# A hybrid attention layer on Trainium2: the gate row summed earlier, the last output block in halves, and loops over pairs of heads written out

## The chip, the cores and the metric

The kernel runs on one core of a Trainium2 chip. The metric is the device time of one execution in microseconds, as a median over runs. Five engines work side by side, each on its own list of instructions, and meet only at semaphores: TensorE (PE, with its weight loads shown as PEld), VectorE (DVE), ScalarE (ACT), GpSimd (POOL) and SyncE (SP), whose queue issues nearly all DMA transfers.

## The reference: what is computed

One decoder layer on x of shape (1, 2048, 1024), all in float32:

```
ada = silu(c) @ w_ada + b_ada;  shift, scale, gate = split(ada, 3)
h = rms_norm(x, norm_w) * (1 + scale) + shift
q_sb, k_sb, v_sb, g_sb, c_q, c_kv, k_rope, g_mla = split(h @ w_in)
A: stick-breaking attention, 8 heads of 64:
   w[t,s] = beta[t,s] * prod over s<j<t of (1 - beta[t,j]), s < t;  beta = sigmoid(q k / 8)
   o_sb = (w @ v) * silu(g_sb)
B: causal softmax attention, 8 heads, q and k of 96 (64 + 32 rotary), v of 64,
   q and kv lifted from latents of 384 and 256, per-head RMS norms of q and k
   o_mla = (softmax(q k / sqrt(96)) @ v) * silu(g_mla)
out = x + gate * (concat(o_sb, o_mla) @ w_out)
```

`gate` is one row of 1024 numbers: silu(c) times the last third of `w_ada`, plus the last third of `b_ada`.

## The kernel before

Four stages follow each other, the first two closed by a barrier of all engines. To keep float32 accuracy at the speed of the rounded type, most operands are split into a high part (a rounded copy, by ScalarE or GpSimd) and a low part (the operand less its high part, by VectorE or GpSimd), and a product is made as three matmuls: high by high, low by high, high by low.

**Features** (`features`, to 416.2 us). The normalised input is turned, split and multiplied with the columns of q, k and both gates. Beside it VectorE forms the products of the gate row (`gate_row`, lines 549 to 560): partition p of the tile `keep` (128 x 1024) holds the sum over k of silu(c)[k*128+p] times row k*128+p of `w_ada`. The sum over the 128 partitions and the bias are still missing.

**Tokens** (`tokens`, lines 723 to 1366, 416.2 to 797.8 us). For each of 16 blocks of 128 tokens: values, latents, lifted q and k, norms, rotary turn, and their transposes. It opens with the weights: SyncE issues the loads (lines 891 to 912), ScalarE casts eight blocks of `w_tok` (line 1003) and then five blocks of the lifting weights (line 1007), VectorE makes the low parts (lines 1108, 1115), and TensorE's first product (`project_v`, line 1278) takes the eight blocks one by one as their low parts come (`s_wl`). The PSUM tile `pq` is first written by the transposes of `latents` for block 0.

**Attention** (`attend`, from 797.8 us). Heads are taken in four pairs, the variable `it`. In both parts a Python planner (`Plan`, `Turns`) lays down the order in which every engine goes through the pair: *units* or *pieces* of 128 x 512 scores, and *turns*, one block of 128 keys for 512 queries. A turn passes from engine to engine through rings of four or eight tiles.

The stick-breaking part (`attend_sb`): TensorE makes scores (line 1799), ScalarE takes a sigmoid (line 1635), VectorE a running product (line 1713); then TensorE transposes (line 1828), ScalarE copies out of PSUM (line 1646), GpSimd makes the high part and the low part for three turns of four (lines 1607 and 1609) and TensorE multiplies with the values (lines 1843, 1844). A pair has 80 units and 80 turns. The helper `pairs` (line 1496) runs pair 0 as written-out code and pairs 1 to 3 as passes of one counted loop, in which each engine jumps back on its own:

```python
def pairs(eng, body):
    body(0, True)
    with eng.Fori(1, PAIRS) as it:
        body(it, False)
```

Waits inside the loop compare a semaphore with a value computed in a register from `it`.

The softmax part (`attend_mla`): TensorE makes scores twice, once to find row maxima (line 2250, `piece`; VectorE reduces them, line 2162) and once transposed (line 2287); ScalarE exponentiates twice (lines 2109, 2110), GpSimd makes the low part (line 2083), VectorE adds up (line 2201), TensorE multiplies with the values (lines 2303, 2304). At the end of a group of 512 queries, ScalarE copies the scale (line 2132), GpSimd multiplies with the SiLU gate (line 2094), VectorE with the scale (line 2224), and high and low parts are stored (line 2033). Its `run` writes out pairs 0 and 3 and loops over pairs 1 and 2, so each engine jumps back once. The code runs straight on from the stick-breaking part, and the first pieces are mixed into its last turns.

**Output** (`output`). Sixteen blocks of 128 rows, last rows first. For each, 48 matmuls into one of two pairs of PSUM banks (line 2453), VectorE multiplies with `keep` (line 2432), GpSimd adds x (line 2422), SyncE stores. SyncE issues the loads of block n+2 (four for the mixed heads, one for x) after the store of block n. Before the first multiply the gate row is finished here: after the last weights of the softmax, TensorE multiplies `keep` with a matrix of ones into the banks of block 1 (line 2438), which sums over partitions and spreads the sum at once; `sync` loads the bias (line 2402) after the last product with the values, behind the loads of x for block 0 and of both inputs of block 1; VectorE adds the two into `keep` (line 2427). TensorE's block 1 waits for that, since its banks hold the sum.

## Time and profile before

| | us |
|---|---|
| median of 3 runs (lowest, highest) | 2006.79 (1998.55, 2008.7) |
| the profiled execution | 2009.26 |
| its span in the trace | 2007.5 |
| PE busy | 1862.4 (93%) |
| DVE busy | 1251.5 (62%) |
| POOL busy | 1029.5 (51%) |
| ACT busy | 950.9 (47%) |
| output stage, from about 1803 us | 204.5 |

Busy shares over the whole span hide that the stages differ; the rows further down give them by stage. In a timeline row the bracket gives the idle time of that engine before the operation and what the profile takes to have ended it. Branches and register instructions are not counted as busy.

### The profile page before, as it was taken

The page shows a single profiled execution, that of the slowest core. Times are in us where ns is not written, and L with a number is a line of the kernel's source. Part 1 is how long each engine was busy: PE and PEld are TensorE (multiplying, and loading weights), DVE is VectorE, ACT ScalarE, POOL GpSimd, SP SyncE. Part 2 cuts the span into 40 slices and gives each one's busy share as a digit, 9 for nine tenths or more (in the row PEclk, how much of TensorE's full clock was granted, in tenths as well). Part 3 has the DMA queues.
Part 4 walks back from the last instruction along what each step waited for, and adds up shares of the span by engine and source line. Part 5 has one row for each costly group of instructions (what it writes and reads, how often), then busy time and mean ns, then how long its engine had stood idle before and what let it go on. Part 6 is the DMA issues. An engine that isn't in the chain of part 4 may idle for free.

```text
span 2007.5 us, 31970 instructions
## 1 busy us (share of the span) xinstructions
PE 1862.4 (93%) x9757; PEld 1545.8 (77%) x9757; DVE 1251.5 (62%) x1875; ACT 950.9 (47%) x1892; POOL 1029.5 (51%) x1038
## 2 busy tenths in 40 slices
PE   7999999979999994799998989799999999987998
PEld 4888888859999993587777767588887887876786
DVE  4742222135555554799989899788988889872010
ACT  2521111133333332477776767577777777770000
POOL 3410000003333433299998989777877878771122
PEclk9999999989999996799999999899999999988999
DMA  7696522344555544631618053514550545315654
GB/s 274 225 315 201 170 89 89 116 179 158 182 180 191 185 160 138 159 85 50 161 38 194 22 148 68 128 46 86 108 123 23 126 94 103 118 43 163 188 183 147
DMA packets 224836, 273.83 MB, mean 136 GB/s; under 512 B 14000, under 2 KB 161744, under 8 KB 219328
## 3 DMA queue, kind: packets, MB, share of 16 engines
q1 hardware_dynamic: 221088, 266.58, 46.8%
q10 hardware_dynamic: 3616, 5.77, 1.0%
q8 instruction: 49, 0.80, 0.2%
q14 instruction: 83, 0.68, 0.1%
HBM read 159.06 MB, written 109.05 MB: 134 GB/s over the span
## 4 chain that ended last, share of the span: by engine, by line
PE 26%; issue 13%; POOL 9%; DVE 5%; DMA 3%; ACT 2%; SPq 1%; POOLq 0%; ACTq 0%; DVEq 0%
PE at_high L2287 8%; POOL sb_wh L1607 3%; PE at_low L2250 3%; DVE sb_w L1713 3%; PE at_b L2303 3%; PE at_low L1799 3%; POOL sb_wl L1609 2%; PE at_b L2304 2%; DMA out_x<-in_x 2%; POOL out_o L2422 2%; PE at_b L1828 2%; POOL wl L2083 1%; PE at_b L2315 1%; PE at_b L1843 1%; PE at_b L1844 1%
## 5 line engine op out<-in xcount | busy, mean ns | idle before, releaser
L2083 POOL TENSOR_TENSOR wl<-w,wh 128x512 fp32r<-128x512 f32 (+1 forms) x320 | 377.6, 1195 | 101.5 <-ACT wh L2110 95.6
L1609 POOL TENSOR_TENSOR sb_wl<-sb_wf,sb_wh 128x512 fp32r<-128x512 f32 (+2 forms) x240 | 286.4, 1193 | 19.2
L1713 DVE TENSOR_TENSOR_SCAN sb_w<-kp,sb_w,at_high 128x512 f32<-128x512 f32 x192 | 245.4, 1278 | 28.1 <-ACT kp L1635 12.6
L2109 ACT ACTIVATE w<-at_high 128x512 f32<-128x512 f32 (+1 forms) x320 | 170.8, 534 | 117.0 <-PE at_high L2287 58.5
L2162 DVE TENSOR_REDUCE nmx<-at_low 128x1 f32<-128x512 f32 (+2 forms) x320 | 191.6, 600 | 7.2 <-PE at_low L2250 4.3
L1635 ACT ACTIVATE kp<-at_low 128x512 f32<-128x512 f32 (+3 forms) x320 | 169.0, 531 | 32.7 <-PE at_low L1802 12.3
L1607 POOL CAST sb_wh<-sb_wf 128x512 fp32r<-128x512 f32 (+2 forms) x240 | 145.7, 607 | 57.3 <-ACT sb_wf L1646 56.8
L663 PE MATMUL pt_po<-h_hi,pt_wl 128*128 128x512 f32 x432 | 170.3, 394 | 0.0
L662 PE MATMUL pt_po<-h_lo,pt_wh 128*128 128x512 f32 x432 | 169.3, 392 | 0.0
L2110 ACT ACTIVATE wh<-at_high 128x512 fp32r<-128x512 f32 (+1 forms) x320 | 169.1, 529 | 0.0
L661 PE MATMUL pt_po<-h_hi,pt_wh 128*128 128x512 f32 x432 | 168.1, 389 | 0.0
L1843 PE MATMUL at_b<-sb_wh,values 128*128 128x512 f32 (+1 forms) x320 | 145.1, 454 | 19.8 <-POOL sb_wl L1609 19.4
L1799 PE MATMUL at_low<-keys,q_hi 128*128 128x512 f32 (+3 forms) x320 | 131.2, 410 | 32.4 <-DMA q_lo<-qk_sb 20.1
L85 POOL MEMSET tk_ident<- 128x128 f32 x1 | 0.2, 204 | 298.0 <-POOLq L64 298.0
L2201 DVE TENSOR_TENSOR at_b<-at_b,w 128x512 f32<-128x512 f32 x168 | 116.8, 695 | 29.6 <-ACT w L2109 26.1
L2250 PE MATMUL at_low<-keys,q_hi 96*128 96x512 f32 (+2 forms) x320 | 124.5, 389 | 10.6 <-DVE nmx L2162 10.5
L2287 PE MATMUL at_high<-q_hi,keys 97*128 97x512 f32 (+1 forms) x320 | 126.0, 394 | 2.5 <-ACT wh L2110 1.9
L1646 ACT ACTIVATE sb_wf<-at_b 128x512 f32<-128x512 f32 (+2 forms) x160 | 88.4, 553 | 77.4 <-PE at_b L1828 75.9
L2303 PE MATMUL at_b<-wh,values 128*128 128x512 f32 (+1 forms) x320 | 124.0, 387 | 0.7 <-POOL wl L2083 0.6
L1828 PE MATMUL at_b<-ident,sb_w 128*128 128x128 f32 x732 | 117.6, 277 | 3.9 <-DVE sb_wl L1722 3.5
L1799 PE MATMUL at_low<-keys,q_lo 128*128 128x512 f32 (+3 forms) x320 | 121.0, 378 | 0.0
L2422 POOL TENSOR_TENSOR out_o<-out_y,out_x 128x1024 f32<-128x1024 f32 x16 | 38.2, 2387 | 159.9 <-DVE out_y L2432 151.4
(266 smaller groups left out, 4658.1 us busy)
## 6 DMA issues: line engine op xcount, KB each, us to landing
qk_mla<-tk_th SPq DMA_DIRECT2D x64, 192.0 KB, 2.1
qk_mla<-tk_tl SPq DMA_DIRECT2D x64, 192.0 KB, 2.4
whole<-in_w_ada SPq DMA_DIRECT2D x8, 1024.0 KB, 14.2
pt_w<-in_w_feat SPq DMA_DIRECT2D x16, 512.0 KB, 6.0
qk_sb<-pt_oh SPq DMA_DIRECT2D x32, 256.0 KB, 3.1
qk_sb<-pt_ol SPq DMA_DIRECT2D x32, 256.0 KB, 4.0
hT<-h_hi SPq DMA_DIRECT2D x16, 512.0 KB, 4.7
hT<-h_lo SPq DMA_DIRECT2D x16, 512.0 KB, 6.2
```

The lines of the kernel that those rows point to most:

```text
L662: nc.tensor.matmul(bank[:], wh[s][:, k, :], hl[:, k, cols_q], start=False, stop=False)
L663: mm = nc.tensor.matmul(bank[:], wl[s][:, k, :], hh[:, k, cols_q], start=False, stop=(k == KD - 1))
L1607: nc.gpsimd.tensor_copy(wh[i][:, lo:GW], wf[i][:, lo:GW]).then_inc(s_phi, 1)
L1609: nc.gpsimd.tensor_tensor(wl[i][:, lo:GW], wf[i][:, lo:GW], wh[i][:, lo:GW].bitcast(F32), ALU.subtract).then_inc(s_plo, 1)
L1713: nc.vector.tensor_tensor_scan(kept, keeps, beside[:, 0:b - a], 1.0 if u["n"] == 0 else w[u["g"]][:, u["r"], b:b + 1], ALU.mult, ALU.bypas ...
L1799: mm = nc.tensor.matmul(out, buf[x][hp][:, q], buf["kk"][hp][:, u["a"]:u["z"]], start=(k == 0), stop=(not masked and k == 1))
L2083: nc.gpsimd.tensor_tensor(wl[i][:, cols], w[i][:, cols], wh[i][:, cols].bitcast(F32), ALU.subtract).then_inc(s_lo, 1)
L2109: nc.scalar.activation(w[i][:, cols], zt[x % 2][:, cols], ACT.Exp).then_inc(s_w, 1)
L2162: nc.vector.tensor_reduce(nmx[pc["n"] % 2][:, pc["r"], pc["c"]:pc["c"] + 1], zn[p % 2][:, 0:pc["width"]], AX.X, ALU.max, negate=True).then ...
L2250: mm = nc.tensor.matmul(zn[p % 2][:, 0:width], qh[hp][0:QK, i * P:(i + 1) * P], kh[hp][0:QK, pc["c"] * GW:pc["c"] * GW + width], start=Tru ...
L2287: mm = nc.tensor.matmul(zt[x % 2][:, lo:GW], a[hp][0:KP, keys], b[hp][0:KP, g * GW + lo:(g + 1) * GW], start=(k == 0), stop=(k == 2 and no ...
L2303: nc.tensor.matmul(out, vj, wh[x % RING][:, lo:GW], start=tn["first"], stop=False)
```

## The change

1. *Gate row.* The sum over partitions moves to the start of the token stage. SyncE loads the last third of `b_ada` as two rows of 512 on one partition, into tiles not yet used, right behind the two head norms and ahead of the weight loads. TensorE, before its first product, adds for each half of the row `ones(128x128) x keep` and `ones(1x128) x bias` in PSUM (`pq`), and ScalarE, between its two groups of weight casts, copies the finished row back into `keep`. The transposes of block 0 wait for that copy. In the output stage the two matmuls, the bias load and the addition go; block 1 waits for the last softmax weights instead.
2. *Loads.* A new `load_second` issues the loads of x for blocks 0 and 1 and of the mixed heads for block 1 as soon as the last scores are made, after the second group's store of the last pair, no longer behind all stores.
3. *Last block.* Block 15 is multiplied in two halves of 512 columns, each through all of k. VectorE multiplies each half with the gate row; GpSimd adds x to the first, VectorE itself to the second; each half is stored by itself.
4. *Pairs.* `pairs`, `run` and both `sync` bodies are Python loops over the four pairs: every pair is written out on every engine, and waits compare with constants. The order of operations within and between pairs is as before.

```diff
--- before.py
+++ after.py
@@ -741,6 +741,7 @@
         dv = m.sb("dv", [P, H * HD])
+        ones = m.sb("ones", [P, P])
         vt = m.sb("vt", [P, H, 2, HD], F32R)
@@ -800,7 +801,13 @@
+        bias = [dv[0:1, :], ln[0:1, 0:512]]
+
         s_ident = m.sem("ident")
+        s_ones = m.sem("ones")
+        s_bias = m.sem("bias")
+        s_gsum = m.sem("gate_sum")
+        s_gate = m.sem("gate")
         s_const = m.sem("const")
@@ -890,6 +897,8 @@
             sp.dma_start(gk[:], t["k_head_norm"].partition_broadcast(P)).then_inc(s_head, 16)
+            for j in range(2):
+                sp.dma_start(bias[j], t["b_ada"][2 * D + j * 512:2 * D + (j + 1) * 512].unsqueeze(0)).then_inc(s_bias, 16)
             for k in range(SLOTS, NS):
@@ -946,6 +955,7 @@
         def _(pool):
+            nc.gpsimd.memset(ones[:], 1.0).then_inc(s_ones, 1)
             make_identity(nc, pool, ident, s_ident)
@@ -1001,6 +1011,8 @@
                 nc.scalar.activation(wh[:, k, :], raw(k % NS), ACT.Copy).then_inc(s_wh, 1)
+            act.wait_ge(s_gsum, 1)
+            nc.scalar.activation(keep[:].rearrange("p (j n) -> p j n", j=2), pq[:], ACT.Copy).then_inc(s_gate, 1)
             for j in range(NW):
@@ -1296,6 +1308,8 @@
                 pe.wait_ge(s_ln, 2 * m_ + 2)
+                if isinstance(m_, int) and m_ == 0:
+                    pe.wait_ge(s_gate, 1)
@@ -1362,6 +1376,14 @@
+            pe.wait_ge(s_ones, 1)
+            for j in range(2):
+                if j == 0:
+                    pe.wait_ge(s_bias, 32)
+                cols = slice(j * 512, (j + 1) * 512)
+                nc.tensor.matmul(pq[:, j, :], ones[:], keep[:, cols], start=True, stop=False)
+                mm = nc.tensor.matmul(pq[:, j, :], ones[0:1, :], bias[j], start=False, stop=True)
+            mm.then_inc(s_gsum, 1)
             pe.wait_ge(s_ident, 2)
@@ -1493,11 +1515,10 @@
-    def pairs(eng, body):
-
-        body(0, True)
-        with eng.Fori(1, PAIRS) as it:
-            body(it, False)
+    def pairs(body):
+
+        for it in range(PAIRS):
+            body(it, it == 0)
@@ -1577,10 +1598,8 @@
-        body(0, True, False)
-        with sp.Fori(1, PAIRS - 1) as it:
-            body(it, False, False)
-        body(PAIRS - 1, False, True)
+        for it in range(PAIRS):
+            body(it, it == 0, it == PAIRS - 1)
         store(PAIRS - 1, 0)
...
@@ -1673,7 +1692,7 @@
                 for n, wraps in plan.due(x, after):
-                    if not (isinstance(it, int) and not 0 <= it - wraps < PAIRS):
+                    if 0 <= it - wraps < PAIRS:
                         body(it - wraps, n)
...
@@ -1993,21 +2012,19 @@
             at_it, at_hp = it + h // 2, h % 2
-            if isinstance(at_it, int) and not 0 <= at_it < PAIRS:
+            if not 0 <= at_it < PAIRS:
                 continue
-    def run(eng, steps, tail):
+    def run(steps, tail):
-        body(0)
-        with eng.Fori(1, PAIRS - 1) as it:
+        for it in range(PAIRS):
             body(it)
-        body(PAIRS - 1)
         for x in range(TAIL + 1):
@@ -2065,11 +2082,11 @@
                     output.load_first(sp)
-
-        body(0, True, False)
-        with sp.Fori(1, PAIRS - 1) as it:
-            body(it, False, False)
-        body(PAIRS - 1, False, True)
+                if last and n == 1:
+                    output.load_second(sp)
+
+        for it in range(PAIRS):
+            body(it, it == 0, it == PAIRS - 1)
         store(PAIRS - 1, G - 1)
...
@@ -2382,6 +2397,12 @@
+    def load_second(sp):
+        sp.wait_ge(*softmax.scored)
+        load_x(sp, 0)
+        load_mix(sp, 1)
+        load_x(sp, 1)
+
     def split_high(act, k):
@@ -2394,23 +2415,22 @@
     def sync(sp):
-        sp.wait_ge(*softmax.scored)
-        load_x(sp, 0)
-        load_mix(sp, 1)
-        load_x(sp, 1)
-        sp.wait_ge(*softmax.pv)
-        sp.dma_start(bgate[:], t["b_ada"][2 * D:3 * D].partition_broadcast(P)).then_inc(s_bgate, 16)
         for stored in softmax.stored:
             sp.wait_ge(s_o, n + 1)
+            if n == NB - 1:
+                sp.dma_start(out[0, rows(n), halves[0]], o[n % 2][:, halves[0]]).then_inc(s_st[n % 2], 16)
+                sp.wait_ge(s_end, 1)
+                sp.dma_start(out[0, rows(n), halves[1]], o[n % 2][:, halves[1]]).then_inc(s_st[n % 2], 16)
+                break
             sp.dma_start(out[0, rows(n), :], o[n % 2][:]).then_inc(s_st[n % 2], 16)
-            sp.wait_ge(s_st[b], 16 * NB // 2)
+            sp.wait_ge(s_st[b], 16 * (NB // 2) + 16 * b)
@@ -2419,44 +2439,54 @@
             reached(pool, s_st[b], 16 * (n // 2))
-            nc.gpsimd.tensor_tensor(o[b][:], y[b][:], x[b][:], ALU.add).then_inc(s_o, 1)
+            cols = halves[0] if n == NB - 1 else slice(0, D)
+            nc.gpsimd.tensor_tensor(o[b][:, cols], y[b][:, cols], x[b][:, cols], ALU.add).then_inc(s_o, 1)
     def vector(dve):
-        dve.wait_ge(s_gate, 1)
-        dve.wait_ge(s_bgate, 16)
-        nc.vector.tensor_tensor(keep[:], po[1][:], bgate[:], ALU.add).then_inc(s_keep, 1)
-        dve.wait_ge(s_keep, 1)
         for n in range(NB):
             reached(dve, s_o, n - 1)
+            if n == NB - 1:
+                for j, cols in enumerate(halves):
+                    dve.wait_ge(s_mm, n + 1 + j)
+                    nc.vector.tensor_tensor(y[n % 2][:, cols], po[n % 2][:, cols], keep[:, cols], ALU.mult).then_inc(s_y, 1)
+                dve.wait_ge(s_y, NB + 1)
+                dve.wait_ge(s_x[n % 2], 16 * (n // 2) + 16)
+                reached(dve, s_st[n % 2], 16 * (n // 2))
+                nc.vector.tensor_tensor(o[n % 2][:, cols], y[n % 2][:, cols], x[n % 2][:, cols], ALU.add).then_inc(s_end, 1)
+                break
             nc.vector.tensor_tensor(y[n % 2][:], po[n % 2][:], keep[:], ALU.mult).then_inc(s_y, 1)
     def tensor(pe):
-        pe.wait_ge(*softmax.weighed)
-        for j in range(2):
-
-            mm = nc.tensor.matmul(po[1][:, j * 512:(j + 1) * 512], ones[:], keep[:, j * 512:(j + 1) * 512],
-                                  start=True, stop=True)
-        mm.then_inc(s_gate, 1)
         pe.wait_ge(*softmax.max)
             if n == 1:
-                pe.wait_ge(s_keep, 1)
+                pe.wait_ge(*softmax.weighed)
             reached(pe, s_y, n - 1)
+
+            def products(k, js):
+                for l, wx in ((0, wh), (1, wh), (0, wl)):
+                    for j in js:
+                        mm = nc.tensor.matmul(po[b][:, halves[j]], ms[b][l][:, k, :], wx[k][:, halves[j]],
+                                              start=(k == 0 and l == 0 and wx is wh),
+                                              stop=(k == KD - 1 and wx is wl))
+                return mm
+
+            if n == NB - 1:
+                for j in range(2):
+                    for k in range(KD):
+                        mm = products(k, (j,))
+                    mm.then_inc(s_mm, 1)
+                break
             for k in range(KD):
                     pe.wait_ge(s_wl, k + 1)
-                for l, wx in ((0, wh), (1, wh), (0, wl)):
-                    for j in range(2):
-                        mm = nc.tensor.matmul(po[b][:, j * 512:(j + 1) * 512], ms[b][l][:, k, :],
-                                              wx[k][:, j * 512:(j + 1) * 512],
-                                              start=(k == 0 and l == 0 and wx is wh),
-                                              stop=(k == KD - 1 and wx is wl))
+                mm = products(k, (0, 1))
             mm.then_inc(s_mm, 1)
-    return Output(sync, gpsimd, vector, tensor, load_first, split_high, split_low)
+    return Output(sync, gpsimd, vector, tensor, load_first, load_second, split_high, split_low)
...
```

## Rows read from the trace of the kernel before

**Rows 1.** Windows by stage: length; busy PE, PEld, DVE, ACT, POOL; PEclk, DMA, GB/s

```profile
797.80:1300.00 502.20, 447.43 (x2521) 351.06 (x2521) 437.39 (x488) 342.17 (x693) 422.77 (x490) 0.95 0.45 105
1300.00:1803.00 503.00, 485.91 (x2664) 412.33 (x2665) 436.42 (x750) 373.14 (x754) 396.38 (x336) 0.98 0.38 89
```

**Rows 2.** Timeline, GpSimd, pair starts: start, length, operation [idle before <-releaser]

```profile
947.26 0.61 POOL L1607 CAST sb_wh<-sb_wf 128x512 fp32r<-128x512 f32 x1
...
1061.07 0.74 POOL L1609 TENSOR_TENSOR sb_wl<-sb_wf,sb_wh 128x256 fp32r<-128x256 f32 x1
1065.83 0.61 POOL L1607 CAST sb_wh<-sb_wf 128x512 fp32r<-128x512 f32 x1 [4.02 <-ACT sb_wf L1646]
...
1182.22 0.61 POOL L1607 CAST sb_wh<-sb_wf 128x512 fp32r<-128x512 f32 x1 [3.99 <-ACT sb_wf L1646]
```

**Rows 3.** Timeline of ScalarE after its jump back

```profile
1028.88 0.28 ACT L1635 ACTIVATE kp<-at_low 128x128 f32<-128x128 f32 x1 [2.13 <-issue]
```

**Rows 4.** Timeline of GpSimd behind ScalarE's jump back

```profile
1029.90 0.61 POOL L1607 CAST sb_wh<-sb_wf 128x512 fp32r<-128x512 f32 x1 [0.87 <-ACT sb_wf L1646]
...
1034.18 0.61 POOL L1607 CAST sb_wh<-sb_wf 128x512 fp32r<-128x512 f32 x1 [0.38 <-ACT sb_wf L1646]
...
1040.69 0.61 POOL L1607 CAST sb_wh<-sb_wf 128x512 fp32r<-128x512 f32 x1 [0.36 <-ACT sb_wf L1646]
```

**Rows 5.** Timeline of ScalarE in the softmax stage: pair ends and eleventh turns

```profile
1425.31 0.59 ACT L2132 ACTIVATE scale<-at_b 64x512 f32<-64x512 f32 x1 [0.50 <-PE at_b L2323]
...
1443.63 0.59 ACT L2110 ACTIVATE wh<-at_high 128x512 fp32r<-128x512 f32 x1
...
1548.62 0.59 ACT L2132 ACTIVATE scale<-at_b 64x512 f32<-64x512 f32 x1 [0.50 <-PE at_b L2323]
...
1568.63 0.59 ACT L2110 ACTIVATE wh<-at_high 128x512 fp32r<-128x512 f32 x1
...
1693.68 0.59 ACT L2110 ACTIVATE wh<-at_high 128x512 fp32r<-128x512 f32 x1
```

**Rows 6.** Timeline of VectorE, the same operation in two pairs

```profile
1428.88 0.68 DVE L2224 TENSOR_TENSOR om<-om,scale 128x512 f32<-128x512 f32 x1
...
1677.04 1.74 DVE L2224 TENSOR_TENSOR om<-om,scale 128x512 f32<-128x512 f32 x1
```

**Rows 7.** Timeline of TensorE, start of the output stage

```profile
1802.87 3.10 PE L2438 MATMUL at_high<-gate_row,ones 128*128 128x512 f32 x4
...
1816.27 0.61 PE L2453 MATMUL at_low<-out_wl,out_ms 128*128 128x512 f32 x2
1826.75 2.05 PE L2453 MATMUL at_high<-out_wh,out_ms 128*128 128x512 f32 x4 [9.87 <-DVE gate_row L2427]
```

**Rows 8.** Timeline of VectorE in the output stage

```profile
1825.38 1.22 DVE L2427 TENSOR_TENSOR gate_row<-at_high,out_bgate 128x1024 f32<-128x1024 f32 x1 [12.47 <-DMA out_bgate<-in_b_ada]
...
1840.69 1.22 DVE L2432 TENSOR_TENSOR out_y<-at_high,gate_row 128x1024 f32<-128x1024 f32 x1 [12.83 <-PE at_high L2453]
1851.57 1.23 DVE L2432 TENSOR_TENSOR out_y<-at_low,gate_row 128x1024 f32<-128x1024 f32 x1 [9.65 <-PE at_low L2453]
...
1999.45 1.23 DVE L2432 TENSOR_TENSOR out_y<-at_high,gate_row 128x1024 f32<-128x1024 f32 x1 [9.65 <-PE at_high L2453]
```

**Rows 9.** Windows, the stretch at the lower clock in the output stage

```profile
1819.00:1832.60 13.60, 5.85 (x14) 4.68 (x15) 2.45 (x2) 0.00 (x0) 2.36 (x1) 0.50 0.56 176
```

**Rows 10.** Timeline of SyncE's queue in the output stage

```profile
1819.21 0.43 SPq L2402 DMA_DIRECT2D out_bgate<-in_b_ada  x1
```

**Rows 11.** Waits of TensorE from 1840 us on: us, times, longest us

```profile
PE at_high L2453 <- DMA out_ms<-mix_mla: 3.9, 4, 1.8
```

**Rows 12.** Timeline of GpSimd, its last add

```profile
2000.76 2.34 POOL L2422 TENSOR_TENSOR out_o<-out_y,out_x 128x1024 f32<-128x1024 f32 x1 [8.49 <-DVE out_y L2432]
```

**Rows 13.** Timeline of SyncE's queue, start of the token stage

```profile
419.90 1.42 SPq L900 DMA_DIRECT2D region<-in_w_tok  x2
```

**Rows 14.** Timeline of TensorE, start of the token stage

```profile
432.40 1.22 PE L1278 MATMUL tk_pv<-tk_wh,hs 128*128 128x512 f32 x2 [3.75 <-DVE tk_wl L1108]
```

More of the change, by code:

```diff
@@ L2146, in scalar @@
         row(0, 0, 0)
-        run(act, dict(row=row, turn=weights, half=v_low, sums=totals, mh=high), lambda x: output.split_high(act, x))
+        run(dict(row=row, turn=weights, half=v_low, sums=totals, mh=high), lambda x: output.split_high(act, x))
     def rows_ahead(act, i):
@@ L2331, in tensor @@
         to_row(0, 0, 0)
[L2332 removed]
+        run(dict(**pieces(pe), pm=to_row, turn=scores, product=product, spread=spread, sum=over_keys), lambda x: None)
     class done:
```

42 lines of the change are left out of this document (19 added, 23 removed).

## Prediction

> **What bounds the kernel now.** I read first the busy time of each engine in the stretches of the stages, where the reader is to see that the two attention stages are not bound alike. In the stick-breaking stage (797.8 to 1300 us) TensorE, VectorE and GpSimd are all busy 84 to 89% of 502 us; in the softmax stage TensorE leads with 486 of 503 us [rows 1]. An idle microsecond of any engine that the others soon wait for is therefore nearly a microsecond of the kernel there. Then I read the timeline around the places where the counted loops start over. GpSimd's cast for a new pair of heads comes at 947.26, 1065.83 and 1182.22; the last two stand behind 4.02 and 3.99 us of idle time, while the passage from pair 0 (already written out) into the loop, at 947.26, shows none [rows 2]. The rows name ScalarE as releaser, but the gap stands only where GpSimd's loop starts over, and as long both times: I read it as GpSimd's own jump back. ScalarE has such a gap too, 2.13 us with the releaser "issue" [rows 3], and GpSimd then waits for it three times, 0.87+0.38+0.36 us [rows 4]. Third, the output stage: TensorE ends block 0 at 1816.27+0.61 and stands idle 9.87 us for the gate row [rows 7], which VectorE could form only at 1825.38, after 12.47 us for the bias, whose load was issued at 1819.21 [rows 8, 10]. Last, the end: multiply (1.23 us), then GpSimd's add (2.34 us), then the store [rows 8, 12].
>
> **Gate row, removed from the output stage.** Three things go. The wait: 9.87 us. The clock: from 1819.0 to 1832.6 the granted clock was 0.50, the 1.2 GHz level, after TensorE had fallen idle [rows 9], so block 1 took from 1826.75 to the multiply at 1840.69, 13.94 us, where block 2 took 1851.57-1840.69 = 10.88 us [rows 7, 8]; 3.06 us come back if block 1 follows block 0 without a pause. The two matmuls with the ones: 3.10 us ahead of block 0 [rows 7]. Block 0 can move up by that at most, and by less where VectorE's weight splits or a lower clock hold it: 0 to 3.1 us, taken 1.4. Together 9.87+3.06+1.4 = 14.3 us at the end of block 1, which then ends near 1826.4. That needs block 1's own loads early: `load_second` issues them when the last scores are made (about 1795), ahead of the third group's store, which is due only at 1807; they are there long before 1815.5. What is late next: the loads for block n+2 follow the sum of block n. Block 2 had them free while TensorE stood idle; now its loads start near 1819.5 and block 1 ends near 1826.4. The same distance cost block 3 1.8 us, the longest of the four waits of that kind, 3.9 us in all [rows 11]. I give back 1.0 us (0 to 3). Net: -13.3 us.
>
> **Gate row, added to the token stage.** SyncE issues two more loads ahead of the weights. One such issue costs 0.43 us [rows 10], so everything behind them on that queue goes out about 0.8 us later, and with it the weight blocks issued at 419.90 [rows 13], for whose low part TensorE waits 3.75 us at 432.40 [rows 14]. That wait is on the path: +0.8 us. The matmuls: two of the same shape took 3.10 us at the lower level [rows 7]; four take up to 6.2 us there and half of that at the upper. They start when the bias is in, near 419.5, while TensorE otherwise has only as much to do as VectorE's weight splits come in; it catches up in the 3.75 us of idle time before 432.40. So their price is nothing; without that cover it would be 3 us. ScalarE copies the row, 128x1024, about 1 us between two groups of weight casts; queued behind it are those casts and the first copy of values, and TensorE needs neither before its next token block. GpSimd's extra memset (0.2 us for a like one on the page) is done before the bias is in. Bounds 0 to +3, taken +0.8 us.
>
> **Pairs of heads written out, stick-breaking.** Two jumps back go on each engine. GpSimd's: 4.02+3.99 us gross [rows 2]. But the trace shows that part of it is given back: the pair that begins after a stall lasts 1182.22-1065.83 = 116.39 us, the one that begins without lasts 118.57 us [rows 2], both with one stall inside; behind the stall the ring is full and GpSimd runs without waiting. So a stall is worth 4.0-2.2 = 1.8 us net, two 3.6 us. ScalarE's: the three waits that it hands to GpSimd are 1.6 us [rows 4], twice 3.2 us. Sum -6.8 us. Bounds: 3 us (if the waits of rows 4 are mostly the ordinary ones) and 2x4.0+2x2.13 = 12.3 us (nothing given back). Register arithmetic that goes with the loop variable I count at nothing: in the softmax stage a looped pair and a written-out one take 125.00 and 125.05 us [rows 5]. The Trainium skill ("Runtime: NRT & Kernel Launch", Instruction fetch mechanics) says that a jump taken to a target outside the two blocks at hand forces a fetch before work goes on, and that straight code is prefetched mostly hidden. By that rule, the trace agrees with 4.0 and 2.1 us at the jumps and none at 947.26; the sum would be the same.
>
> **The same, softmax stage.** One jump back goes, at 1548.7. A pair without one lasts 1548.62-1425.31 = 123.31 us. From the eleventh turn of one pair to that of the next it is 1568.63-1443.63 = 125.00 us with the jump and 1693.68-1568.63 = 125.05 us without it [rows 5]. So the jump costs 1.7 us, but the following pair lost as much without one: there VectorE's multiply of two SBUF operands took 1.74 us in place of 0.68 [rows 6]. Whether the freed pair runs like the first or like the last I can't tell: -1.7 to 0, and to the loss side +1.7 if another pair falls into that pattern. Taken -0.8 us. The Trainium skill ("SBUF — State Buffer", SBUF: two separate sides) has a rule that speaks against a clean gain here: VectorE with two SBUF inputs and GpSimd hold one port pair exclusively, and the later one waits for the whole instruction. By that rule, the trace agrees with 1.74 against 0.68 us; timing alone decides which pair pays.
>
> **Last block in halves.** From the last matmul to the store: now 1.23 us, then GpSimd's add to 2003.10, 3.65 us after 1999.45 [rows 8, 12]. After: VectorE multiplies half a row (0.7 us) and adds the half itself (two SBUF operands of 128x512, 0.68 us without a neighbour [rows 6]; GpSimd's half is done 5 us earlier), with hand-over 1.5 us: -2.2 us. The last transfer is half as large: 0 to 1 us, no row shows this size, taken 0.4. TensorE's count of matmuls and weight loads is the same in either order. Sum -2.6 us.
>
> **Sum.** -13.3+0.8-6.8-0.8-2.6 = -22.7 us. The profiled execution took 2009.26 us (span 2007.5): 1986.6. From the median of the runs, 2006.79, it is 1984.1. I say 1985.
>
> **Rivals.** (a) The jumps are absorbed or return as other stalls in straight code, and only the output stage gains: 2006.79-15.1 = 1991.7 us. For it: all three engines are near 88%, so the next limit is near. Against: pair 0 of either stage. (b) Nothing is given back in the stick-breaking stage and the softmax pair is freed: 12.3+1.7 for 7.6 us, 1977.7 us. Against: 118.57 and 116.39. (c) The change doesn't do what it says in the output stage: block 1's loads come as late as now (about 1822), TensorE pauses 6.5 us, and the lower clock level stays, 3 us: 1993.6 us. Against: SyncE has nothing else to wait for at 1795. (d) Slower: the code itself becomes the bound. Five pairs that were loop passes are now new code on every engine; if GpSimd stalled in straight code as it does at a jump, 4.0 us, twice in each, that is 40 us against 15.1, 2032 us. It decides from the eighth stall on (25 us above the output's gain). Against: pair 0 of the stick-breaking stage and the last softmax pair run straight without a gap of that kind.
>
> **How the numbers follow.** Forecast 0.60 (its own range 1980 to 1990), (a) 0.17, (b) 0.12, (c) 0.05, (d) 0.03, and 0.03 for mixtures near no change. A measurement here can tell about 0.5%, 10 us, from no change; the runs shown spread from 1998.55 to 2008.7. Faster: all but (d) and the mixtures, and a little of (c): 0.93; same 0.04; slower 0.03. The range takes in (a), (b) and the bounds of the token stage: 1973 to 1996.
>
> **What would show it.** Right: in the changed profile GpSimd's gaps of 4.0 us near 1061 and 1178 are gone, the pairs of the stick-breaking stage are 113 to 114 us apart, block 1 of the output starts within 0.5 us of block 0's end at clock 1.0, and the last store follows TensorE by about 2.2 us. Wrong: gaps of 2 to 4 us on GpSimd or ScalarE inside straight pairs (d), pairs still 116 us or more apart (a), a DMA wait before block 1 (c), or the token stage longer by over 3 us.

## The result, and the profile after

The changed kernel takes 1976.79 us (median of 4 runs, 1971.02 to 1983.54) where the kernel before, on the same chip, takes 2007.74 us (4 runs, 1998.55 to 2008.7). The ratio is 0.9859, with a 95% interval of 0.9832 to 0.9885: 23 to 34 us less. The profiled execution took 1976.82 us with a span of 1975.1, which is 32.4 us less than the span before. The forecast was 22.7 us less, given as 1985 us.

By stage, the windows of after that answer to [rows 1] (length, then busy time of PE, PEld, DVE, ACT and POOL, then granted clock, DMA share, GB/s; moved so that they begin with the same work):

```profile
790.00:1285.00 495.00, 443.51 (x2517) 348.05 (x2517) 436.89 (x487) 342.10 (x691) 423.47 (x489) 0.95 0.46 108
1285.00:1782.00 497.00, 481.73 (x2653) 408.31 (x2653) 433.45 (x745) 371.27 (x752) 397.17 (x336) 0.99 0.39 90
1800.00:1811.00 11.00, 11.00 (x50) 8.90 (x48) 1.22 (x1) 0.00 (x0) 2.39 (x1) 1.00 0.57 173
```

The engines do the same work in the stick-breaking stage (443.5 against 447.4 us of TensorE, 436.9 against 437.4 of VectorE) in less time. What went is idle time. The third line is block 1 of the output: TensorE is busy without a pause and at the upper clock level, where [rows 9] showed 0.50.

GpSimd at the starts of the four pairs, which answers to [rows 2] (start, length, operation, idle time before it and its releaser):

```profile
835.26 0.61 POOL L1626 CAST sb_wh<-sb_wf 128x512 fp32r<-128x512 f32 x1 [38.35 <-ACT sb_wf L1665]
...
944.30 0.61 POOL L1626 CAST sb_wh<-sb_wf 128x512 fp32r<-128x512 f32 x1
...
1056.72 0.61 POOL L1626 CAST sb_wh<-sb_wf 128x512 fp32r<-128x512 f32 x1
...
1169.20 0.61 POOL L1626 CAST sb_wh<-sb_wf 128x512 fp32r<-128x512 f32 x1
```

The casts at 1056.72 and 1169.20 have no bracket: the gaps of 4.02 and 3.99 us are gone. The pairs are 112.42 and 112.48 us apart, where it was 118.57 and 116.39.

VectorE in the output stage, which answers to [rows 8]:

```profile
1800.31 1.22 DVE L2458 TENSOR_TENSOR out_y<-at_low,gate_row 128x1024 f32<-128x1024 f32 x1 [3.03 <-PE at_low L2472]
1811.19 1.22 DVE L2458 TENSOR_TENSOR out_y<-at_high,gate_row 128x1024 f32<-128x1024 f32 x1 [9.65 <-PE at_high L2472]
...
1969.87 0.69 DVE L2452 TENSOR_TENSOR out_y<-at_high,gate_row 128x512 f32<-128x512 f32 x1 [4.65 <-PE at_high L2472]
1970.59 0.69 DVE L2456 TENSOR_TENSOR out_o<-out_y,out_x 128x512 f32<-128x512 f32 x1
```

Blocks 0 and 1 are multiplied 10.88 us apart, the distance of two undisturbed blocks. The last multiply starts at 1969.87. SyncE issues the last store 1.44 us after it, where the last add of before ended 3.65 us after its multiply [rows 8, 12]:

```profile
1966.62 0.34 SPq L2423 DMA_DIRECT2D out<-out_o  x1
1971.31 0.33 SPq L2425 DMA_DIRECT2D out<-out_o  x1
```

**One pair of profiles is not enough.** Cut at the same instructions, the profile after is 1.66 us ahead at the first weight remainder of the token stage already, 415.79 against 417.45 us. The diff changes nothing before that point. Over all fourteen profiles of this study that moment lies between 415.66 and 418.76 us, in kernels whose code is the same up to there (one, e11, has its loops there written out: 417.82). So the terms below are taken as means over profiles that have, or lack, the piece in question.

### The profile page after: what moved, and what is told of

The parts are those of the page before. It is cut to its first block, busy times and chain, and to the rows that moved or that the text cites. A ratio compares the mean times of both kernels' runs of the same rounds, so it can differ in the third digit from the quotient of the medians.

```text
span 1975.1 us, 29422 instructions
## 1 busy us (share of the span) xinstructions
PE 1856.5 (94%) x9761; PEld 1538.4 (78%) x9761; DVE 1251.6 (63%) x1876; ACT 953.3 (48%) x1893; POOL 1031.9 (52%) x1039
## 4 chain that ended last, share of the span: by engine, by line
PE 25%; issue 11%; POOL 10%; DVE 10%; DMA 2%; ACT 1%; SPq 1%; POOLq 0%; ACTq 0%; DVEq 0%
PE at_high L2304 8%; DVE sb_w L1732 6%; POOL sb_wl L1628 4%; PE at_low L2267 3%; POOL sb_wh L1626 3%; PE at_b L2320 3%; PE at_b L2321 2%; POOL wl L2100 2%; PE at_low L1818 2%; DMA out_x<-in_x 2%; POOL out_o L2443 2%; PE at_b L2332 1%; PE at_b L1847 1%; PE at_b L1862 1%; SPq L2386 1%
## 5 line engine op out<-in xcount | busy, mean ns | idle before, releaser
L1863 PE MATMUL at_b<-sb_wl,values 128*128 128x512 f32 (+1 forms) x320 | 117.9, 369 | 0.0
```

## Experiments

Each kernel gets a median and a ratio to the kernel before, timed on the same chip. The medians of before were 2005.63 (e1 to e4), 2004.72 (e5 to e8) and 2006.38 us (e9 to e12). From each profile I also take the same seven distances, starts of instructions read off the timelines:

- **token**: VectorE's first `tk_wl` to TensorE's last high-part matmul (`tk_wh`) into `tk_pv`
- **stick**: ScalarE's first `kp` to GpSimd's last cast `sb_wh`
- **softmax**: GpSimd's first to its last `wl`
- **block 1**: that last `wl` to the multiply of the output's second block
- **blocks**: from there to the multiply of the 15th block
- **tail**: from there to the start of the last instruction on record
- the first moment (**start**), 415.66 to 418.76 us throughout

```
kernel              token   stick  softmax  block 1  blocks   tail    span
before             326.47  482.82   491.92    43.98  147.88  18.90  2007.5
e1_loops_both      326.74  473.64   489.09    42.36  146.88  19.28  1995.2
e2_loops_stick     326.71  473.40   489.78    42.30  146.19  18.99  1993.1
e3_loops_softmax   326.71  480.52   488.36    42.76  146.93  18.90  2000.8
e4_output_part     326.19  480.48   492.44    27.98  145.23  16.22  1983.2
e5_stick_pool      327.12  478.58   493.94    42.26  146.04  18.92  2001.8
e6_stick_scalar    327.06  479.08   487.50    41.43  146.28  19.20  1993.3
e7_gate_old_loads  325.14  484.90   489.47    37.81  147.16  16.18  1997.0
e8_halves_alone    326.97  483.52   488.92    41.44  147.65  16.91  2001.1
e9_warm_only       325.60  481.00   490.12    42.32  146.15  18.99  1999.1
e10_token_small    326.94  473.17   490.12    28.99  146.29  16.25  1974.3
e11_all_loops_out  325.00  474.37   489.06    29.21  146.07  16.48  1975.8
e12_after_again    325.37  473.70   489.63    29.17  146.88  16.08  1974.3
after              325.37  473.93   489.36    28.39  147.32  16.54  1975.1
```

### The loops alone: e1, e2, e3

```
-        body(0, True)
-        with eng.Fori(1, PAIRS) as it:
-            body(it, False)
+        for it in range(PAIRS):
+            body(it, it == 0)
```

This is done on all five engines (SyncE's loop has its last pass apart) in both stages (e1), in the stick-breaking stage (e2) or in the softmax stage (e3).

> The kernel before, with the loops over the pairs written out on all five engines in both attention stages and nothing else changed. By the theory as predicted (each jump gives back about half of its stall, the softmax stage almost nothing): -7.6 us, about 2000.1. By the rival read from the two traces (8.5 us in the stick-breaking stage, 4.3 in the softmax stage): -12.8 us, about 1995. If the loops' part of the difference were a chance of the profiled runs, under 5 us.

> The kernel before, with the pairs written out in the stick-breaking stage alone. As predicted: -6.8 us, about 2000.9; distances of the first casts of pairs on GpSimd 113 to 114 us throughout. By the traces: -8.5 us, about 1999.2, with distances 109, 112.4, 112.5, 115.2.

> The kernel before, with the pairs written out in the softmax stage alone. As predicted: -0.8 us, about 2006.9. By the traces: -4.3 us, about 2003.4. If the 4.3 us of the softmax stage came instead from when that stage starts (the clock in its first turns), the change is the 1.1 to 2.3 us of the jump behind pair 1 alone.

Measured: e1 1995.67 us, ratio 0.9950 [0.9933, 0.9968]; e2 1994.63 us, 0.9947 [0.9930, 0.9964]; e3 2003.49 us, 0.9993 [0.9983, 1.0004]. The stick-breaking stage gives 7 to 14 us by e2's ratio. By the distances it takes 473.7 us on average in the six profiles with all its engines written out (473.17 to 474.37) and 482.2 in the six with all looped (480.48 to 484.90): -8.5 us. The prediction's -6.8 and the traces' -8.5 can't be told apart by the times; the mean of the distances speaks for 8.5. The looped stage also scatters by 4.4 us, the written-out one by 1.2. In the softmax stage the two profiles compared first had suggested -4.3 us by their shifts. The expectation built on that, -12.8 us for e1 and -4.3 for e3, missed: e1 is 10.0 us below before by medians and e3 2.1, and e3's interval takes in 1, so its time alone can't be told from nothing. The mean distance is 489.3 us written out (six profiles) and 490.5 looped (eight, 487.50 to 493.94): -1.2 us, inside the scatter of the looped ones.

### The output's part alone: e4

The change without its loops (diff as shown ahead of the prediction, all but `pairs`, `run` and SyncE's two bodies).

> The kernel before with the gate row's sum in the token stage, the output's loads earlier and the last block in halves; the loops over pairs kept as they are. As predicted: +0.8 in the token stage, -13.3 at block 1, -2.6 at the end: -15.1 us, about 1992.6. By the traces: -1.1 in the token stage, -13.9 and -0.6 in the blocks, -2.3 at the end: -17.9 us, about 1989.8.

Measured: 1984.93 us, ratio 0.9901 [0.9882, 0.9919], so -16 to -24 us. The traces' -17.9 lies inside that, the prediction's -15.1 just outside; by medians it is -20.7. The expectation read from the two traces, -17.9, was thus the nearer one. Block 1's multiply comes 27.98 us after the last `wl` where before had 43.98 and the eight profiles with the old gate row 42.4 on average. Together with e1 it gives -30.7 us by medians, and after has -31.0: the two parts add up.

### One engine's loop alone: e5, e6

```
-        pairs(pool, body)
+        pairs(pool, body, (pool,))
```

In e5 this line writes out the stick-breaking loop on GpSimd alone, in e6 the like line on ScalarE alone.

> The kernel before, with the pairs of the stick-breaking stage written out on GpSimd alone; ScalarE, VectorE, TensorE and SyncE keep their loops. As predicted (each of the two GpSimd jumps is worth 4.0 us and 2.2 come back): -3.6 us for the stage, from its first turn to the last pair's last cast 480.5 us (the looped profiles of e3 and e4) to about 476.9. Rival: the engines' jumps stand in each other's cover, so that with one of them left nothing is won: 480.5 stays. Second rival: GpSimd's is the only one that counts: the whole 6.8, 473.7.

> The kernel before, with the pairs of the stick-breaking stage written out on ScalarE alone. As predicted (1.6 us at each of two jumps): -3.2 us, the stage 480.5 to about 477.3. Rivals: nothing, 480.5, if GpSimd's jump right behind it sets the pace anyway; the whole 6.8, 473.7, if ScalarE's is the only one that counts. Together with the run before it: if the two add up to about 6.8, the jumps count one after the other; if both are near nothing, they cover one another.

Measured: e5 2000.35 us, ratio 0.9969 [0.9956, 0.9982]; e6 2000.56 us, 0.9975 [0.9965, 0.9985]. Each gains alone, so the stalls don't cover one another; neither gains all. The stage takes 478.58 and 479.08 us, 3.6 and 3.1 below the mean of the six looped profiles, 482.2 (one profile each, and the looped ones reach down to 480.48). The gains foreseen were 3.6 and 3.2; but the expectations started from 480.5, and their end points, 476.9 and 477.3, were missed by 1.7 and 1.8 us. GpSimd in e6, where ScalarE has no jump and GpSimd still has:

```profile
1056.58 0.74 POOL L1613 TENSOR_TENSOR sb_wl<-sb_wf,sb_wh 128x256 fp32r<-128x256 f32 x1
1061.82 0.61 POOL L1611 CAST sb_wh<-sb_wf 128x512 fp32r<-128x512 f32 x1 [4.50 <-issue]
...
1177.27 0.61 POOL L1611 CAST sb_wh<-sb_wf 128x512 fp32r<-128x512 f32 x1 [4.78 <-issue]
```

Here the profile names no releaser but "issue": nothing was waited for. That is not because ScalarE's loop is gone. In e7, further down, every engine has its loop, and the same gap is 4.61 us at both jumps and reads "issue" as well:

```profile
1066.26 0.61 POOL L1629 CAST sb_wh<-sb_wf 128x512 fp32r<-128x512 f32 x1 [4.61 <-issue]
```

Over the six profiles with all engines looped the gap ranges from 3.35 to 5.00 us. What settles whose gap it is are the branch records of the loop's own line, which the timeline leaves out. GpSimd in before, in the window 1060:1067:

```profile
L1499 POOLq COMPARE_BRANCH  x1: 50/50/50, 1061.1 to 1061.1; - x1
L1499 POOLq FUSED_REGOPS  x1: 55/55/55, 1065.5 to 1065.5; - x1
```

GpSimd branches at 1061.1, and its next instruction of any kind, one that only computes in registers, starts at 1065.5: 4.4 us, spent before any arithmetic on the loop variable. Between 1061.0 and 1065.5 the profile lists two transfers on a queue of the kind "instruction" (16 KB together). So the gap is GpSimd's jump, whatever releaser [rows 2] names. ScalarE's branch is followed by 2.4 us of nothing at the same kind of place; VectorE's by 0.3 us (1026.1 to 1026.4), and at the softmax stage's jump GpSimd's too (1548.7 to 1549.0). So a jump back is not always dear.

In e5 the places are swapped. First GpSimd, then ScalarE:

```profile
1060.43 0.74 POOL L1613 TENSOR_TENSOR sb_wl<-sb_wf,sb_wh 128x256 fp32r<-128x256 f32 x1
1061.62 0.61 POOL L1611 CAST sb_wh<-sb_wf 128x512 fp32r<-128x512 f32 x1 [0.44 <-ACT sb_wf L1650]
...
1178.59 0.61 POOL L1611 CAST sb_wh<-sb_wf 128x512 fp32r<-128x512 f32 x1 [0.63 <-ACT sb_wf L1650]
```

```profile
1028.50 0.28 ACT L1639 ACTIVATE kp<-at_low 128x128 f32<-128x128 f32 x1 [2.10 <-issue]
```

The distances of GpSimd's casts at the pair starts, and from the last of them to the stage's last cast, show how the gain comes about (us; means of six profiles in the first two lines, one profile in the others):

```
                       pair 0   pair 1   pair 2   pair 3
all engines looped      109.4    118.6    116.2    113.3
all written out         109.0    112.5    112.6    114.7
e5, GpSimd written out  109.3    114.6    114.4    115.5
e6, ScalarE written out 109.0    117.4    115.4    112.4
```

Pairs 1 and 2 end in a jump where they are looped. In e5 pair 1 is 3.9 us shorter than looped, pair 2 is 1.8 shorter and the last pair 2.2 longer. So each later pair does give back about half of the stall before it, as the prediction priced it.

### Where the output's loads stand: e7

Against e4:

```
                 if last and n == 0:
                     output.load_first(sp)
-                if last and n == 1:
-                    output.load_second(sp)
...
     def sync(sp):
+        load_second(sp)
         for stored in softmax.stored:
```

> As e4 (gate row in the token stage, last block in halves, loops kept), but the loads of block 1 and of the two x blocks stand where they were, ahead of the output's own issues instead of behind the second last store of the softmax stage. If the moved loads are needed for the pause of block 1 to go, this kernel loses against e4: the loads come about as late as the last stored group's issue lets them, some 3 to 9 us at block 1 (1988 to 1994 against e4's 1984.9). If block 1's data is early either way, it is equal to e4 within 1 us.

Measured: 1996.97 us, ratio 0.9944 [0.9924, 0.9964], against e4's 0.9901. By the two ratios that is 0.43% or 8.6 us worse than e4, at the slow end of the 3 to 9 us expected; by the medians 12.0, more than the 1988 to 1994 us expected. Block 1's multiply comes 37.81 us after the last `wl`, 9.8 later than in e4. The chain, SyncE's queue and TensorE, and VectorE's two multiplies:

```profile
1810.72 0.33 SPq L2055 DMA_DIRECT2D mix_mla<-mh  x1
1811.10 0.43 SPq L2055 DMA_DIRECT2D mix_mla<-ml  x1
1811.57 0.46 SPq L2395 DMA_DIRECT2D out_x<-in_x  x1
1812.07 0.45 SPq L2391 DMA_DIRECT2D out_ms<-mix_sb  x1
```

```profile
1820.65 2.07 PE L2478 MATMUL at_high<-out_wh,out_ms 128*128 128x512 f32 x4 [7.44 <-DMA out_ms<-mix_mla]
```

```profile
1813.25 1.23 DVE L2464 TENSOR_TENSOR out_y<-at_low,gate_row 128x1024 f32<-128x1024 f32 x1 [2.62 <-PE at_low L2478]
1833.61 1.22 DVE L2464 TENSOR_TENSOR out_y<-at_high,gate_row 128x1024 f32<-128x1024 f32 x1 [19.14 <-PE at_high L2478]
```

The loads stand in the queue behind the last stores of the softmax stage, go out at 1812, and TensorE idles 7.44 us for them. The two multiplies are 20.36 us apart instead of 10.88: 9.5 us, the pause and 2.0 us behind it; from TensorE's restart at 1820.65 to 1824.40 the granted clock is 0.50, and then 1.00. In after the same six loads go out from 1779.37 on:

```profile
1779.37 0.46 SPq L2390 DMA_DIRECT2D out_x<-in_x  x1
1779.87 0.46 SPq L2386 DMA_DIRECT2D out_ms<-mix_sb  x1
```

So two thirds of the gain at block 1 hang on six moved issues. Without them the gate row's removal mostly uncovers the next late arrival.

### The last block in halves: e8

Before with the last block's matmuls, multiply, add and store in two column halves, and nothing else:

```
+            if n == NB - 1:
+                for j in range(2):
+                    for k in range(KD):
+                        mm = products(k, (j,))
+                    mm.then_inc(s_mm, 1)
+                break
```

> The kernel before, with only the last block of the output computed, added and stored in halves. As predicted -2.6 us, and by the profiles of after and e4 -2.8 (from the last block's first y to the end 5.18 instead of 8.02, less what the reordering of its matmuls costs): about 2003.0 against 2005.6 of before. If the halves' gain were taken back by the second half's store, within 0.5 us of before.

Measured: 2002.26 us, ratio 0.9986 [0.9974, 0.9997]: -0.6 to -5.2 us. The tail is 16.4 us on average in the seven profiles with halves and 19.0 in the seven without: -2.65 us.

### The four extra matmuls of the token stage: e9, e10

Here the profile contradicts the prediction's sign: the token stage was to take 0.8 us longer and took 1.1 less. TensorE at its start, in after:

```profile
417.63 2.05 PE L1384 MATMUL tk_pq<-gate_row,tk_ones 128*128 128x512 f32 x2 [8.21 <-DMA tk_ln<-in_b_ada]
419.61 2.07 PE L1385 MATMUL tk_pq<-tk_dv,tk_ones 1*128 1x512 f32 x2
421.61 2.08 PE L1384 MATMUL tk_pq<-gate_row,tk_ones 128*128 128x512 f32 x2
423.62 2.07 PE L1385 MATMUL tk_pq<-tk_ln,tk_ones 1*128 1x512 f32 x2
425.62 1.22 PE L1290 MATMUL tk_pv<-tk_wh,hs 128*128 128x512 f32 x2
...
432.36 0.63 PE L1290 MATMUL tk_pv<-tk_wh,hs 128*128 128x512 f32 x2
```

The matmuls take 8.0 us in all and fill the time in which TensorE would wait for weights. The projection then starts late, with its weights at hand, and never waits: the pause of 3.75 us at 432.40 [rows 14] is gone, and the length of a group falls from 1.22 to 0.63 us once the clock is up. The granted clock, in windows of before, of after, and of e10 (last columns as in [rows 1]):

```profile
412.00:429.50 17.50, 7.52 (x18) 4.39 (x18) 8.52 (x7) 6.81 (x6) 1.12 (x7) 0.71 0.65 239
429.50:440.00 10.50, 7.60 (x33) 6.68 (x34) 7.87 (x8) 7.41 (x8) 0.00 (x0) 0.66 0.58 223
```

```profile
412.00:429.50 17.50, 11.87 (x17) 5.11 (x18) 8.51 (x7) 8.20 (x8) 1.26 (x8) 0.51 0.75 261
429.50:440.00 10.50, 10.50 (x62) 9.77 (x62) 7.54 (x8) 6.60 (x8) 0.00 (x0) 1.00 0.50 189
```

```profile
412.00:429.50 17.50, 7.25 (x20) 5.23 (x20) 8.71 (x7) 8.40 (x8) 1.26 (x8) 0.71 0.72 264
429.50:440.00 10.50, 9.68 (x41) 8.78 (x42) 7.84 (x9) 5.86 (x8) 0.00 (x0) 0.67 0.48 186
```

In after the clock is the lower level (1.2 GHz, 0.51) while the extra matmuls run and the upper one (1.00) from 429.5 on, for all of the second window. In e9, next, it is 0.99 there as well:

```profile
412.00:429.50 17.50, 13.16 (x20) 6.08 (x21) 8.37 (x7) 6.81 (x6) 1.26 (x8) 0.62 0.64 240
429.50:440.00 10.50, 8.73 (x47) 7.40 (x47) 7.88 (x8) 7.42 (x8) 0.00 (x0) 0.99 0.53 211
```

In before and in e10 it rises early, for part of the first window, falls back after TensorE has waited for weights, and stands at 0.66 and 0.67 on average in the second, where the work waits for TensorE.

e9 takes the kernel before and adds only matmuls (and the tile of ones that they read):

```
+            pe.wait_ge(s_ones, 1)
+            for j in range(2):
+                cols = slice(j * 512, (j + 1) * 512)
+                nc.tensor.matmul(pq[:, j, :], ones[:], keep[:, cols], start=True, stop=False)
+                nc.tensor.matmul(pq[:, j, :], ones[0:1, :], keep[0:1, cols], start=False, stop=True)
             pe.wait_ge(s_ident, 2)
```

> The kernel before with four matmuls of the gate sum's shapes at the start of the token stage whose sums nobody reads (the second of each pair takes a row of the gate sums in place of the bias): no bias loads, no copy, no wait, and everything else as before. By the theory that TensorE's work ahead of the first projection lifts its clock sooner, the token stage (from VectorE's first weight remainder to the first kp of the stick-breaking stage) falls from 396.0 us, the mean of seven profiles with the gate row in the output, to about 394.6, and the time by about 1.4. By the prediction's view (the matmuls hidden, nothing won) 396.0. If they delay the first projection: 397 to 400.

e10 takes after and shrinks them (and ScalarE's copy) to 64 columns. It leaves the gate row unfinished, so its output is not the layer's and only its times are used:

```
-                nc.tensor.matmul(pq[:, j, :], ones[:], keep[:, cols], start=True, stop=False)
-                mm = nc.tensor.matmul(pq[:, j, :], ones[0:1, :], bias[j], start=False, stop=True)
+            mm = nc.tensor.matmul(pq[:, 0, 0:64], ones[:], keep[:, 0:64], start=True, stop=True)
```

> The kernel after with the gate row's sum in the token stage shrunk to one matmul of 64 columns and a copy of 64 columns (the rest of the gate row is then left as it was, so the sum over blocks and the bias are left out); the bias loads, the waits and the output stay. By the clock theory the token stage goes back from 394.6 to about 396 us or a little more (the two bias issues remain): about +1.5 against after. If it was not the matmuls that shortened the stage, it stays at 394.6.

Measured: e9 2002.29 us, ratio 0.9982 [0.9972, 0.9992]: 1.6 to 5.6 us less, from matmuls whose result nobody reads. The stage as the expectation cuts it, to the first `kp`, takes 325.60+68.38 = 393.98 us against 396.0. e10 1975.75 us, where after (e12, beside it) has 1975.99: the times don't tell the two apart, and the stage in that cut takes 394.93 against 394.25 and 394.66, not the 396 expected. The cut was too wide: its last part, from TensorE's last `tk_pv` to the first `kp`, varies between 67.9 and 69.9 us with no regard to the matmuls. Without it (the column token) the picture is clean: 325.0 to 326.2 us in the six profiles with the four full matmuls, 326.5 to 327.1 in the seven of kernels without them, and 326.94 in e10. So the matmuls shorten the stage by 1.4 us (e9's one profile: 1.2, a little under what its ratio gives).

The traces also tell the clock's part from the waits' part. The product that follows the projection (`tk_pl`) and the first group of the next projection, in after and then in e10:

```profile
433.06 0.78 PE L1303 MATMUL tk_pl<-tk_wh,hs 128*128 128x384 f32 x4
...
440.42 0.63 PE L1290 MATMUL tk_pv<-tk_wh,tk_hs 128*128 128x512 f32 x2
```

```profile
433.21 1.32 PE L1303 MATMUL tk_pl<-tk_wh,hs 128*128 128x384 f32 x4
...
442.01 0.63 PE L1290 MATMUL tk_pv<-tk_wh,tk_hs 128*128 128x512 f32 x2
```

Both kernels begin their token stage within 0.01 us of each other (415.79 and 415.80), and at the first `tk_pl` e10 is only 0.15 us behind, although its projection had paused 4.99 us for weights: up to there the four extra matmuls of after and the pauses of e10 come to the same. Over the next product, in which TensorE waits for nothing in either, the lag grows to 1.59 us, since e10 is at the lower clock level until 436.4 (groups of 1.32 us) and after is not (0.78 us). So 1.4 of the 1.6 us between the two are the clock.

### All loops written out, and after again: e11, e12

e11 also replaces the counted loops of the feature stage (two on ScalarE, one on TensorE) and the token stage's loop over block pairs on every engine, as:

```
-            with eng.Fori(FIRST // 2, NB // 2 - 1) as i:
+            for i in range(FIRST // 2, NB // 2 - 1):
```

> The kernel after with the last loops of the program written out too: four in the stage of features and the loop over block pairs of the token stage on every engine. A candidate. By the stick-breaking stage (3 to 4 us for each of its two jump places) up to -8; but in these stages the engines wait more for one another and the jumps lie beside other work, so -1 to -3 us is what I expect, against after in the same call. Rival: nothing, within 1 us; or slower, if more instructions have to be fetched in a straight line.

> The kernel after as it is, for its segments in a second profile and for its time beside the two kernels made from it. About 1975 to 1977 us; stick-breaking stage 473.7, softmax stage 489, token stage 394.6, from the last wl to the second y 28.4 (all within 1 us of the first profile of after, if its segments are typical).

Measured: e11 1978.23 us, ratio 0.9852 [0.9834, 0.9869]; e12 1975.99 us, 0.9845 [0.9830, 0.9861]. The candidate wins nothing (the token column is 0.4 us shorter, which is within its scatter) and costs nothing that can be told; the best version stays the changed kernel. Expected were -1 to -3 us; the rival, nothing, holds. (The expectation speaks of four loops in the feature stage; there are three.) e12 repeats the segments of after within 0.8 us, so those are typical.

## Why the prediction was right, and where its sizes were off

The mechanism was right at every step but the token stage's, and the reading of one softmax pair was wrong besides; the sum was 5 us too small. The time, 1976.8, lies in the wide range of 1973 to 1996 but outside the forecast's own 1980 to 1990, and nearest to rival (b). Measured terms are differences of the column means over profiles that have the piece and that lack it.

```
term                          predicted   measured
gate row out, block 1             -14.3      -13.6
given back in later blocks         +1.0       -0.3
last block in halves               -2.6      -2.65
token stage                        +0.8       -1.4
pairs, stick-breaking stage        -6.8       -8.5
pairs, softmax stage               -0.8       -1.2
sum                               -22.7      -27.7
```

The medians differ by 29 to 31 us (1976.79 and 2007.74, 1975.99 and 2006.38), so some 2 to 3 us are left that the means don't place; the start and the looped stages alone scatter by more than that between executions. The profiled pair differs by 32.4 because before's profile has a late start (0.4 us behind the mean of fourteen, after's is 1.3 ahead of it) and long softmax and output columns.

**Token stage: the wrong sign, the clearest miss, 2.2 us.** "So their price is nothing" was argued from cover alone, and the delay of the weights was taken as on the path: "+0.8 us". SyncE's two bias issues did stand ahead of the weights, and TensorE did wait for the bias until 417.63. But the same rows said what the step missed: [rows 14] shows 1.22 us for a matmul group at that place, the lower level's length, beside a 3.75 us wait. The granted clock in before is 1.00 from 422.9 to 426.3 and 0.50 from there to 436.5, past a pause of 1.77 us before 425.58 and this one of 3.75, and the product behind the weights runs its first part at the lower level. Work put into the idle time changed that, and the first product behind the weights ran at the upper level. e9 shows that it is the matmuls (ratio below 1, token 325.60), e10 that without them the stage is back at 326.94 and by which way (the clock). A size was off too: "four take up to 6.2 us" rests on 3.10 us "at the lower level" for two, but the granted clock over those 3.10 us of [rows 7] was 0.61 on average, and at the lower level the four took 8.0.

**Stick-breaking stage: right mechanism, 1.7 us too small.** The bounds were 3 and 12.3. The single-engine runs agree with both prices, 3.6 and 3.1 us against 3.6 and 3.2, though with one profile each. All five engines together give 8.5. By the pair distances the missing 1.8 us lie at the two jumps, about 1 us each: pairs 1 and 2 shorten by 6.1 and 3.6 us, where e5 and e6 add up to 5.1 and 2.6. Either the jumps of VectorE, TensorE and SyncE, counted at nothing, are worth it (about 0.3 us each on record, so only if they add up without overlap), or the stall left on one engine keeps part of what the other frees, or the looped stage's scatter (4.4 us between profiles) makes it. No run tells these apart. The distances "113 to 114 us" came out as 112.42 and 112.48, and the stage's last cast then comes 114.5 to 115.2 us after the first one of its pair in the six written-out profiles, where the six looped ones have 112.4 to 114.3 (mean 113.3): 1 to 2 us of the gain is given back in the last pair.

**Softmax stage: within its bounds.** VectorE's multiply at the pairs' ends, 1.74 against 0.68 us in before, takes the long form at all three pair ends of after:

```profile
1416.22 1.75 DVE L2241 TENSOR_TENSOR om<-om,scale 128x512 f32<-128x512 f32 x1
...
1541.03 1.75 DVE L2241 TENSOR_TENSOR om<-om,scale 128x512 f32<-128x512 f32 x1
...
1664.96 1.75 DVE L2241 TENSOR_TENSOR om<-om,scale 128x512 f32<-128x512 f32 x1
```

So all three fell into the long form and still the stage did not get longer. The prediction put the last pair's 125.05 us down to this multiply. The other runs don't bear that out: in e8 it takes 1.74 us at the same place, and that pair takes 122.74 us. What made the pair of before long stays open. A mean of -1.2 us with looped profiles between 487.5 and 493.9 is no more than "about as predicted".

**Output: right.** The loads went out before the softmax stage's last stores, at 1779.37, as the step needs them to. The gate row's 14.3 us came as 13.6. e7 confirms rival (c)'s price: with the loads in their old place the prediction gave a pause of 6.5 us and 3 us of clock, 9.5 in all; measured were 7.44 and 9.5 in all. Of the +1.0 given back, block 2's new wait is 0.43 us, and the waits on the whole did not grow. The waits for mix blocks from block 2 on are what they were (the rows that answer to [rows 11]; us, times, longest):

```profile
PE at_high L2472 <- DMA out_ms<-mix_mla: 3.6, 4, 1.7
PE at_low L2472 <- DMA out_ms<-mix_mla: 0.3, 1, 0.3
```

Before had one such `at_low` wait too, of 0.7 us. I had treated block 2's load as a new collision; it is one more wait of a kind that other blocks had, and one of them lost its own. The tail went as worked out: multiply to store 1.44 us (1.5 predicted), columns 19.03 to 16.38.

**Rivals.** (a) fell with e1 and e2: the jumps' time is gone, not moved. (b) named the right time, 1977.7, but by luck: it took 12.3 us from the stick-breaking stage with nothing given back, where 8.5 came and part of each stall is given back (e5: 4.0 us of gap removed twice, 3.6 gained); the token stage and what the means don't place make up the rest. For (c) see e7. (d) fell: in after GpSimd and ScalarE show no "issue" gap at the pair borders, and e11, with still more straight code, takes the same time within its interval. (Its threshold is off: 25 us of stalls of 4.0 us are passed with the seventh, not the eighth.)

## What to carry to other kernels

Look at an engine's idle time where its loop starts over, and don't believe the releaser's name there: a gap at every pass that is missing at the first is a sign of the jump, and the records of the branch and of the next instruction decide it (4.4 us here). Its worth is the gap less what a full ring behind it gives back. Jumps differ: at others only 0.3 us were lost. When an edit removes the last wait of a stage, price the next arrival with its issue's place in the queue; here six moved issues carried two thirds of the gain. Matmuls added where TensorE idles at the lower clock level had a negative price here: ask what the clock does behind them, and measure a term of 1 us over the shortest stretch that holds it, in several profiles.

## What the runs showed of the hardware that I had not expected

- Four matmuls whose result nobody reads made the kernel faster (e9, ratio 0.9982 [0.9972, 0.9992]): 8.0 us of them in an idle stretch, and the granted clock from 429.5 to 440 us was 0.99 where it had been 0.66. Between after and e10 nearly all of the difference is the clock: `tk_pl`, begun within 0.15 us of each other, took 7.36 and 8.80 us.
- The gap at GpSimd's jump in the stick-breaking stage is 3.35 to 5.00 us over the six looped profiles (4.50 and 4.78 in e6), ScalarE's there 2.03 to 2.31; at GpSimd's softmax jump 0.3 us pass between branch and next instruction. What decides between the two is not shown; before lists two transfers of the kind "instruction" in the long gap at 1061 us. In the token stage the loops' removal brought 0.4 us (e11), within the scatter. That other waits cover the jumps there is my reading; it wasn't tested.
- Executions of the same code reach the token stage at 415.7 to 418.8 us. One pair of profiles can't place a difference of 2 us.
